# Recurrent chunks and the attention half of the first merge in one loop of units, slots as a plain ring, loops written out

## The reference

```
h = rmsnorm(x)
q, k, v, xr, gr, g_attn, g_rnn = split(h @ w_in)           # 7 parts of 1024 columns
attn_out = diff_attention(q, k, v, ...)                    # 8 heads
gate = gelu(gr)
xc = conv4(xr)                                             # 4 taps over the tokens
r, i = sigmoid(xc_block @ w_rg_a + b), sigmoid(xc_block @ w_rg_x + b)   # 8 blocks of 128
a = exp(-8 * r * softplus(-lam));  b = sqrt(1 - a*a) * (i * xc)
h_t = a_t * h_(t-1) + b_t                                  # scan over the tokens
rnn_out = h * gate
merged = sigmoid(g_attn) * (attn_out @ w_proj_attn) + sigmoid(g_rnn) * (rnn_out @ w_proj_rnn)
x = x + merged @ w_out
x = x + square(relu(rmsnorm(x) @ w_up)) @ w_down
# second block: forget-gate attention (fox), window attention (swa), short convolution,
# a merge of three branches (merge2), cross attention, a gated feed-forward part
```

## Time and profile before

| what | us |
|---|---|
| median of 3 runs | 2279.29 (2279.01 to 2282.69) |
| span of the profiled execution (its own time, first to last instruction) | 2276.7 |
| TensorE matmuls busy | 2090.8 (92%) |
| VectorE busy | 1026.6 (45%) |
| ScalarE busy | 494.8 (22%) |
| GpSimd busy | 1214.2 (53%) |
| DMA | 186.26 MB, mean 82 GB/s |

### The profile page before, as it was taken

The page is one execution under the profiler, slowest core; times in us unless marked ns, Lnnn a source line. Parts: engine busy times, 40 slices in busy tenths (PEclk is TensorE's granted clock), DMA queues, the critical chain, the costliest instruction groups (busy, mean ns, idle before and its releaser), DMA issues.

```text
span 2276.7 us, 26964 instructions
## 1 busy us (share of the span) xinstructions
PE 2090.8 (92%) x9207; PEld 1657.6 (73%) x9207; DVE 1026.6 (45%) x1445; ACT 494.8 (22%) x991; POOL 1214.2 (53%) x1003
## 2 busy tenths in 40 slices
PE   6499997678999999999799989899999889999997
PEld 4366665567887888888667767688878878888886
DVE  6155555884116412215755564443365455313124
ACT  4144443441002201102123222111022121101012
POOL 2233314547665666666423431367775756767663
PEclk9699997889999999999899988899999999999999
DMA  3412311123332333332311421133343333333321
GB/s 91 136 55 64 100 41 53 52 77 92 93 100 80 98 93 93 99 95 65 93 28 35 104 56 46 42 83 97 105 117 93 91 87 96 97 93 101 94 84 55
DMA packets 347573, 186.26 MB, mean 82 GB/s; under 512 B 14749, under 2 KB 341571, under 8 KB 347508
## 3 DMA queue, kind: packets, MB, share of 16 engines
q1 hardware_dynamic: 343188, 179.60, 27.7%
q10 hardware_dynamic: 4320, 5.77, 0.8%
HBM read 183.18 MB, written 8.45 MB: 84 GB/s over the span
## 4 chain that ended last, share of the span: by engine, by line
PE 79%; DVE 11%; issue 3%; ACT 3%; DMA 2%; POOL 0%; SPq 0%; DVEq 0%; ACTq 0%; POOLq 0%
PE bank L628 22%; PE bank L630 22%; PE bank L632 22%; PE bank L746 3%; PE bank L723 2%; DMA RAW<-in_w_in 1%; DMA bias_tiles_l<-bias_rows_l 1%; PE bank L712 1%; PE bank L694 1%; PE bank L778 1%; DVE HS L1687 1%; DVE HS L1686 1%; DVE XC L1657 1%; PE bank L934 1%; DVE GT L1681 1%
## 5 line engine op out<-in xcount | busy, mean ns | idle before, releaser
L595 POOL TENSOR_TENSOR WL<-RAW,WH 128x1024 fp32r<-128x1024 f32 (+3 forms) x331 | 807.5, 2439 | 27.7
L628 PE MATMUL bank<-HH,WH 128*128 128x512 f32 x1560 | 636.1, 408 | 81.8 <-DVE GT L1549 41.9
L632 PE MATMUL bank<-HH,WL 128*128 128x512 f32 x1560 | 628.8, 403 | 0.0
L630 PE MATMUL bank<-HL,WH 128*128 128x512 f32 x1560 | 626.4, 402 | 0.0
L591 POOL TENSOR_TENSOR gate<-gate 128x1 f32<-128x1 f32 x331 | 80.2, 242 | 1004.2 <-PE bank L632 933.3
L628 PEld LDWEIGHTS bank<-HH,WH 128*128 128x128 f32 x1560 | 303.0, 194 | 152.4 <-issue 54.4
L630 PEld LDWEIGHTS bank<-HL,WH 128*128 128x128 f32 x1560 | 303.1, 194 | 62.1 <-issue 3.1
L632 PEld LDWEIGHTS bank<-HH,WL 128*128 128x128 f32 x1560 | 301.9, 194 | 63.0 <-issue 1.7
L592 POOL TENSOR_SCALAR WH<-RAW 128x1024 fp32r<-128x1024 f32 (+3 forms) x331 | 341.0, 1030 | 0.0
L1722 DVE TENSOR_TENSOR X<-X,bank 128x512 f32<-128x512 f32 x80 | 55.0, 687 | 217.3 <-PE bank L632 217.3
L1549 DVE TENSOR_TENSOR GA<-bank,RSTD 128x512 f32<-128x512 f32 x40 | 27.6, 691 | 222.2 <-PE bank L632 222.0
(11 more groups left out here) (396 smaller groups left out, 3279.4 us busy)
## 6 DMA issues: line engine op xcount, KB each, us to landing
RAW<-in_w_in SPq DMA_DIRECT2D x107, 512.0 KB, 3.8
RAW<-in_w_up SPq DMA_DIRECT2D x32, 512.0 KB, 4.0
RAW<-in_w_down SPq DMA_DIRECT2D x32, 512.0 KB, 3.7
RAW<-in_w_ffn_gate SPq DMA_DIRECT2D x22, 512.0 KB, 3.8
RAW<-in_w_ffn_up SPq DMA_DIRECT2D x22, 512.0 KB, 3.9
RAW<-in_w_xkv SPq DMA_DIRECT2D x16, 512.0 KB, 3.9
RAW<-in_w_ffn_down SPq DMA_DIRECT2D x16, 512.0 KB, 4.0
RAW<-in_w_proj_attn SPq DMA_DIRECT2D x8, 512.0 KB, 3.6
```

The source lines that it names most:

```text
L595: nc.gpsimd.tensor_tensor(WL[:, s, 0:k, :], RAW[:, s, 0:k, :], WH[:, s, 0:k, :].bitcast(F32), ALU.subtract).then_inc(S_[f"unit_cut{s}"], 1)
L628: mm(psum[s][:, 0:n], WH[:, s, k, :], hi(k), start=(k == 0), stop=False)
L630: mm(psum[s][:, 0:n], WH[:, s, k, :], lo(k), start=False, stop=False)
L632: last = mm(psum[s][:, 0:n], WL[:, s, k, :], hi(k), start=False, stop=(k == tiles - 1))
```

## The change

1. The slots are no longer written down per phase: the units of the whole program are numbered, and unit number k uses slot k mod 4 (class `Units`).
2. Between the gate products of chunk n and those of chunk n+1, TensorE now makes xr(n+1), the attention gate of merge column n, the product of AO for column n, and gr(n+1). VectorE takes the gate into GA after HS(n), and writes MG[n] = (tanh + 1) * bank once ScalarE's tanh is there; sigmoid(g) is 0.5 * (1 + tanh(g/2)), and the 0.5 is applied when MG is cut. merge1 keeps two units per column, the recurrent gate and the product of RO, adds them into MG, and cuts MG column by column.
3. GA, SG, GT and G2 lie in buffers of the norms (SQ1, ACC1, STD1); AT and MT are gone (RT and TT are overwritten), so the exponential now waits for the tanh that reads RT.
4. All `Fori` loops are written out; counters are constants.

```
+    ("first", 1, [8, 8]),
+    ("rnn", DC - 1, [2, 8, 8, 8, 8]),
+    ("rnn_last", 1, [2, 8, 8]),
+    ("merge1", DC, [8, 8]),
+    ("merge2", DC, [8, 8, 8, 8, 4]),
...
     def use(self, name, it, j):
+        n = self.place[name, it, j]
+        return n % SLOTS, n // SLOTS + 2
...
             # SP
+            load("first", 0, 0, cols(w["w_in"], D * 3))
+            load("first", 0, 1, cols(w["w_in"], D * 4))
+            for n in range(DC - 1):
+                load_gates("rnn", n, 0)
+                load("rnn", n, 1, cols(w["w_in"], D * 3 + (n + 1) * P))
+                load("rnn", n, 2, cols(w["w_in"], D * 5 + n * P))
+                load("rnn", n, 3, cols(w["w_proj_attn"], n * P))
+                load("rnn", n, 4, cols(w["w_in"], D * 4 + (n + 1) * P))
...
             # TensorE
-            with pe.Fori(1, DC - 1) as n:
-                for j in range(2):
-                    run(from_h("rnn", n, j))
-                rnn_gates(n)
...
+            for n in range(DC):
+                rnn_gates(n)
+                if n < DC - 1:
+                    run(from_h("rnn", n, 1))
+                run(from_h(*rnn_unit(n, 2 if n < DC - 1 else 1)))
...
+                run(from_pair(*rnn_unit(n, 3 if n < DC - 1 else 2), AO))
+                if n < DC - 1:
+                    run(from_h("rnn", n, 4))
+            for e in range(DC):
+                run(from_h("merge1", e, 0))
...
+                run(from_pair("merge1", e, 1, RO))
...
             # VectorE, at the end of a chunk
+                take(*rnn_unit(n, 1 if last else 2), scaled(GA))
                 dve.wait_ge(S_["ro_hi"], n + 1)
                 V.tensor_tensor(RO[1][:, bass.ds(n, 1), :], HS[:].unsqueeze(1),
                                 RO[0][:, bass.ds(n, 1), :].bitcast(F32), ALU.subtract).then_inc(S_["ro_lo"], 1)
+                dve.wait_ge(S_["sg"], n + 1)
+                take(*rnn_unit(n, 2 if last else 3), lambda bank: V.scalar_tensor_tensor(
+                    MG[:, n, :], SG, 1.0, bank[:], ALU.add, ALU.mult))
```

More of the change, by code:

```diff
@@ L506, in _ @@
             load("fgate", 0, 0, cols(w["w_in_2"], C_FORGET))
-            with sp.Fori(0, 4) as h:
+            for h in range(0, 4):
                 for j in range(3):
@@ L525, in _ @@
             wb = w["w_branch_2"]
-            with sp.Fori(0, DC) as e:
+            for e in range(0, DC):
                 load("merge2", e, 0, cols(wb, e * P))
@@ L596, in cut @@
                                         ALU.subtract).then_inc(S_[f"unit_cut{s}"], 1)
-            for name, iters, slots, _t in PHASES:
-                if iters == 1:
-                    for j in range(len(slots)):
-                        cut(name, 0, j)
-                else:
-                    with pool.Fori(0, iters) as it:
-                        for j in range(len(slots)):
-                            cut(name, it, j)
+            for name, it, j in units.order:
+                cut(name, it, j)
         @block.tensor
@@ L868, in _ @@
             mlp_group(0, True)
-            with pe.Fori(1, 3) as g:
+            for g in range(1, 3):
                 mlp_group(g)
@@ L926, in _ @@
             pe.wait_ge(S_["f_out_taken"], 9)
-            with pe.Fori(0, DC) as e:
+            for e in range(0, DC):
                 s, c = units.use("merge2", e, 0)
@@ L1239, in _ @@
             squares(0, True)
-            with act.Fori(1, 3) as g:
+            for g in range(1, 3):
                 squares(g, False)
@@ L1292, in fox @@
                 out_hi2("f", YF, h)
-            with act.Fori(0, 3) as h:
+            for h in range(0, 3):
                 fox(h, False)
@@ L1335, in _ @@
             act.preload_act_table(ACT.Sigmoid)
-            with act.Fori(0, DC) as e:
+            for e in range(0, DC):
                 for j in range(3):
@@ L1750, in _ @@
             mlp_group(0)
-            with dve.Fori(1, 3) as g:
+            for g in range(1, 3):
                 mlp_group(g)
@@ L1881, in fox @@
                 take(*following, 2, scaled(M2["VR"][:]))
-            with dve.Fori(0, 3) as h:
-                own.enter(h, 8)
+            for h in range(0, 3):
                 fox(h, False)
-                own.leave(3)
             fox(3, True)
```

262 lines of the change are left out of this document (110 added, 152 removed).

## The result

| kernel | median, us | runs | ratio to before | 95% interval |
|---|---|---|---|---|
| before | 2279.15 | 4 (2276.52 to 2282.69) | | |
| changed | 2220.78 | 4 (2213.31 to 2224.17) | 0.9744 | 0.9722 to 0.9765 |

The change makes the kernel 2.6% faster, 58 us. The forecast was 2239, with a range from 2222: the direction and the main mechanism held, and the gain was 18 us larger than forecast, just outside the range. The profiled execution of the changed kernel has a span of 2222.4 us.

What follows compares the result with a forecast made beforehand. TensorE bounds nearly everywhere, but VectorE's chain bounds the rewritten stretch. Span 2276.7 - 53.7 (stretch) + 13 (second merge) = 2236.0; with the median 2.6 above the span, 2239 us, range 2222 to 2268.

Steps and rivals of the forecast that it cites:

- The lost 74 us of the stretch: From first attention's end to w_out's first products: TensorE takes 340.9 us for 267 of matmuls; the change gains 53.7 us.
- The start: Between attention and the first gates: TensorE idles 9.3 us instead of 5.0 waiting for XCL, plus 3 at lower clock.
- ROL: After the last gates, before the first product of RO: TensorE waits 2.0 us (0 to 6), like 2.2 before.
- I take 24.4: VectorE's chain per recurrent chunk, us, against TensorE's 23.4; so TensorE waits 1.0 us for the attention gate's take, six times.
- the proportion: GpSimd's disturbance of VectorE per chunk grows with its work, 4.8 to 9.0 us; with 16.2 undisturbed, chain 25.2 us.
- A: Recurrent chunks: VectorE's chain outgrows TensorE more, 27.4 us per chunk; total 2260 us; chance 0.22.
- B: Recurrent chunks: every microsecond of GpSimd's cuts delays VectorE, 32.3 us per chunk; total 2294, slower than before; chance 0.08.
- Rival E: Second merge: unit 0's bank is emptied in time, so the forecast loss of 13 us doesn't occur; total 2226; chance 0.05.
- No loops: I count zero: Whole kernel: removing branches and register arithmetic of 40 TensorE iterations saves nothing (bounds -6 and 0).
- rival C: Whole kernel: leaving out loops saves 0.5 us per iteration x 40 = 20 us; total 2219; chance 0.05.
- rival D: Whole kernel: the added unrolled code must be fetched and is waited for, 26 us; total 2265; chance 0.05.
- Other ring phases keep a distance of four units or get looser: Slot rotation outside the second merge: no term in the sum; unit 0 of swa no longer waiting for its cut left out.

## Why the prediction came out as it did

**The lost 74 us of the stretch: right, and a little more.** Forecast -53.7 up to w_out, measured -52.3 and -7.0, that is -59.3. The start (9.3 forecast, 9.4 measured) was right. So was ROL (2.0, 2.5), but with luck: the kernel with the earlier take in merge2 waited 4.7 us at that place with the same code up to there. The step that failed is the chain of VectorE: "I take 24.4", hence "6 waits, 6 us". The chain was 23.4 us at most, and no wait came. VectorE's 21.6 busy us less the undisturbed durations of its operations (some 12.8) are 8.8 us of disturbance, where 8.2 had been taken and 9.0 came from the proportion. The base of 16.2 us was too large: it was 14.5. It held 0.55 us of links in the loop, which the change took out by unrolling, and a scan of 2.10 us that I had read as undisturbed; it takes 1.23:

```profile
444.09 1.23 DVE L1684 TENSOR_TENSOR_SCAN HS<-AT,MT 128x512 f32<-128x512 f32 x1
```

That row is from the kernel with loops written out. The size of the disturbance was luck as well. With the scan's 0.87 counted in, it was 5.7 us before and not 4.8, and the same proportion then gives 10.7 us and a chunk of some 26: twice the cuts did not cost twice as much. Rivals A and B fell: 16 us of cuts cost 8.8. (A counts 13 operations with both inputs in SBUF; the list has 12.)

But the margin was thin: with 2.2 us more per chunk the waits were there. And the 59.3 us are not all the new order's: 16 of them, by the traces above, come from the missing loops and the ring, which the prediction had at nothing in this stretch. The bounds given, 0 and 24 us, were fair; the middle was taken a microsecond too high.

**Merge2: right.** 11.8 us of waits and 14.2 us of stage for 13 forecast, and the earlier take gave 13 us back. Rival E fell.

**"No loops: I count zero": wrong in size and in place.** Unrolling alone gave 13 us. I had looked for the cost on TensorE, where none is seen (rival C as priced, 0.5 us per iteration, fell too). By the traces 7.6 us of it lie in the cross attention, where the cuts meet other operations, and 2.6 are what is left of the gain at VectorE's links once the wait before RO has grown. The Trainium skill ("Runtime: NRT & Kernel Launch", Instruction fetch mechanics) says that kernels prefer full unrolling, since a taken branch can stall the engine. Unrolling gained here, but no stall at a branch was seen on TensorE. No wait for fetched code showed, so rival D fell.

**"Other ring phases keep a distance of four units or get looser", left out: wrong.** Looser was worth 26 us by the medians; by the traces 6 at the forget gate and 13 from the end of the attention to w_out. The rest is within the spread of the runs. The order of units in the old table had two places at which a unit waited for its slot or bank: the forget gate's, right behind the MLP's last unit in the same slot, and unit 1 of merge1. They could have been found by listing the distance between two uses of a slot at every joint of phases, and the first of them by this one of TensorE's waits in the trace of before, between 1085 and 1115 us, the end of the MLP:

```profile
PE bank L628 <- POOL WL L595: 3.8, 1, 3.8
```

**The sum.** Left out or mis-sized, in the trace: stretch -5.6, merge2 +1.2, attention +1.9, forget gate -6.6, fox +5.5, before merge2 -4.9, cross -6.2 and +1.1 for the rest, together -13.6; another 4 us are the medians, which lie 2.5 above the profiled span before and 1.6 below it after.

## What to carry to other kernels

When the operations of one engine are lengthened by another's, look first at how long one instruction of the background engine is: cutting GpSimd's two-input operation in four gave 54 us for a few lines, nearly as much as the whole change. When a reordering fills one engine's idle time, count the other engine's chain from undisturbed durations and add the disturbance after, and measure its room with one and with three dummy operations: the pace of 23.37 us looked the same with VectorE nearly full and with 8 us to spare. Split what they cost into waits and slower matmuls before dividing it by the work added. When slots are assigned in rotation, list for each unit how many units ago its slot and its bank were last used; here a joint with distance one cost some 6 us once, and a take that came one product late 1.5 us in each of eight rounds.

## What the hardware showed unexpectedly

- A VectorE operation with both inputs in SBUF that meets GpSimd's cut ends about 0.5 us after that one instruction does (IT 451.07 to 453.96, WL 450.70 to 453.41), a one-input cut included (STD 449.58 to 451.15, WH 449.56 to 450.61). GpSimd is lengthened in turn (WL 3.17 instead of 2.70 us at 464.71 in the changed kernel). A take that reads a bank is not: ACC at 447.52 took 0.68 us while WL ran from 446.54 to 449.26.
- Four pieces of the same cut took 2.84 us together where no such operation met them, and up to 4.96 where some did (2.70 in one piece), and lowered VectorE's total busy time from 1037.2 to 932.7 us. The Trainium skill ("SBUF — State Buffer", Who interferes with whom) calls the port pair that the two engines share an exclusive lock. The rows above bear that out, operation by operation; that the length of the single GpSimd instruction is what counts is read from the pieces.
- VectorE's scaling of XPR, with one tensor input and one scalar, was lengthened too (2.33 us in the cross attention of before, 0.35 at best).
- Some of VectorE's waits on counts computed in a loop cost 0.16 to 0.22 us, others in the same chunk 0.03; those on constants cost some 0.03 (453.61 + 0.55 to 454.19).
- Idle times of 2.5 us (before RO) and eight of 1.47 (merge2) left TensorE's granted clock at 1.00, the 9.4 us wait before the first gates did not: it was at half, 1.2 GHz, until 377.1 us. Beside the wait of 4.7 us before RO in the kernel with the earlier take it was at half for 6.8 us (mean 0.57 from 558 to 566).
